# Scores of the fine levels of a chunked recurrence: four 32 by 32 products per block of 128 tokens in place of one 128 by 128 product

## The reference, cut to what matters

```python
def step(state, inp):
    q_, k_, v_, b_ = inp          # b_: cumulated log decay
    diff = jnp.where(causal[:, :, None], b_[:, :, :, None, :] - b_[:, :, None, :, :], -jnp.inf)
    a = jnp.einsum('bhtd,bhtsd,bhsd->bhts', q_, jnp.exp(diff), k_)
    o = a @ v_ + jnp.einsum('bhtd,bhde->bhte', q_ * jnp.exp(b_), state)
    ...
```

## Time and profile before

| | |
|---|---|
| three runs | 3310.64, 3315.96, 3316.32 us; median 3315.96 |
| profiled execution, its own time | 3312.84 us |
| its span, first to last instruction | 3311.0 us |
| mean granted TensorE clock | 0.996 |
| the stage of the change in the span | 2310.5 to 2364.4 us |

### The profile page before, as it was taken

The page is one execution under the profiler, slowest core; times in us unless marked ns, Lnnn a source line. Parts: engine busy times, 40 slices in busy tenths (PEclk is TensorE's granted clock), DMA queues, the critical chain, the costliest instruction groups (busy, mean ns, idle before and its releaser), DMA issues.

```text
span 3311.0 us, 48046 instructions
## 1 busy us (share of the span) xinstructions
PE 3235.8 (98%) x16228; PEld 2607.4 (79%) x16228; DVE 1928.3 (58%) x2441; ACT 1718.1 (52%) x2077; POOL 1338.8 (40%) x675
## 2 busy tenths in 40 slices
PE   8999999999999999999999999999989999999998
PEld 7888887678888788888778888778766788888784
DVE  4335684663355433461373333357667899999898
ACT  5552334545533555331445542523463788888884
POOL 3444442044444444444224444434301454445441
PEclk9999999999999999999999999999999999999999
DMA  3225331022244222443422223223103999999997
GB/s 128 95 97 165 125 105 58 8 91 99 95 146 152 83 95 95 141 157 108 131 86 95 95 96 96 100 82 106 59 9 125 367 377 384 388 388 388 371 368 303
DMA packets 128450, 534.38 MB, mean 161 GB/s; under 512 B 24433, under 2 KB 24689, under 8 KB 100465
## 3 DMA queue, kind: packets, MB, share of 16 engines
q1 hardware_dynamic: 107488, 499.63, 42.2%
q0 software_dynamic: 20736, 33.60, 2.7%
q10 hardware_dynamic: 144, 0.08, 0.0%
HBM read 531.64 MB, written 41.94 MB: 173 GB/s over the span
## 4 chain that ended last, share of the span: by engine, by line
PE 71%; issue 15%; POOL 5%; DVE 5%; DMA 3%; ACT 1%; POOLq 0%; DVEq 0%; SPq 0%; ACTq 0%
PE ps L881 20%; PE ps L883 20%; PE ps L882 20%; POOL w_lo L2099 5%; DMA big<-in_exp_gu 2%; PE ps L1448 2%; PE ps L1070 1%; PE ps L901 1%; PE ps L1080 1%; PE ps L1095 1%; DMA big<-slot_rows 1%; DVE hid L2870 1%; PE ps L1541 1%; PE ps L1200 1%; PE ps L1238 1%
## 5 line engine op out<-in xcount | busy, mean ns | idle before, releaser
L2099 POOL TENSOR_TENSOR w_lo<-stage_buf,w_hi 128x1024 fp32r<-128x1024 f32 (+1 forms) x396 | 968.6, 2446 | 1327.1 <-ACT w_hi L1629 1327.0
L1629 ACT ACTIVATE w_hi<-stage_buf 128x1024 fp32r<-128x1024 f32 (+1 forms) x396 | 414.1, 1046 | 1177.9 <-PE ps L883 1125.3
L881 PE MATMUL ps<-x_hi,w_hi 128*128 128x512 f32 x1984 | 773.4, 390 | 5.2 <-POOL w_lo L2099 3.3
L883 PE MATMUL ps<-x_hi,w_lo 128*128 128x512 f32 x1984 | 772.0, 389 | 0.0
L882 PE MATMUL ps<-x_lo,w_hi 128*128 128x512 f32 x1984 | 771.9, 389 | 0.0
L881 PE MATMUL ps<-hid,w_hi 128*128 128x512 f32 x1312 | 518.4, 395 | 3.0 <-issue 1.7
L883 PE MATMUL ps<-hid,w_lo 128*128 128x512 f32 x1312 | 511.6, 390 | 0.0
L882 PE MATMUL ps<-hid,w_hi 128*128 128x512 f32 x1312 | 510.8, 389 | 0.0
L881 PEld LDWEIGHTS ps<-x_hi,w_hi 128*128 128x128 f32 x1984 | 372.3, 188 | 86.7 <-POOL w_lo L2099 5.4
L883 PEld LDWEIGHTS ps<-x_hi,w_lo 128*128 128x128 f32 x1984 | 372.4, 188 | 77.9
L882 PEld LDWEIGHTS ps<-x_lo,w_hi 128*128 128x128 f32 x1984 | 372.4, 188 | 76.8
(11 more groups left out here) (404 smaller groups left out, 4783.6 us busy)
## 6 DMA issues: line engine op xcount, KB each, us to landing
stage_buf<-in_gu SPq DMA_DIRECT2D x176, 512.0 KB, 3.2
big<-in_exp_gu SPq DMA_DIRECT2D x72, 1024.0 KB, 12.0
h_buf<-in_exp_gu SPq DMA_DIRECT2D x72, 1024.0 KB, 12.0
s_buf<-in_exp_dn SPq DMA_DIRECT2D x72, 1024.0 KB, 11.1
stage_buf<-in_down SPq DMA_DIRECT2D x64, 512.0 KB, 3.6
stage_buf<-in_down SPq DMA_DIRECT2D x32, 384.0 KB, 3.2
sil_buf<-in_ada SPq DMA_DIRECT2D x24, 512.0 KB, 4.2
tmp_buf<-in_ada SPq DMA_DIRECT2D x24, 512.0 KB, 4.4
```

The source lines that it names most:

```text
L881: nc.tensor.matmul(o, a_hi, b_hi, start=start, stop=False)
L883: return nc.tensor.matmul(o, a_lo, b_hi, start=False, stop=stop)
L1629: nc.scalar.activation(w_hi[s][:, 0:n], stage[s][:, 0:n], ACT.Copy).then_inc(upper_done, 1)
L2099: nc.gpsimd.tensor_tensor(w_lo[s][:, 0:n], stage[s][:, 0:n], w_hi[s][:, 0:n].bitcast(F32), ALU.subtract).then_inc(parted, 1)
```

## The change

Where r is below 5, a block's 128 by 128 product becomes four products of 32 keys by 32 queries, on the diagonal of the block: 16 products per step in place of 4. The contraction stays 128 channels deep. Their outputs go to PSUM partitions 0, 32, 64 and 96, and cover the 32 by 32 squares on the diagonal; the rest of the bank keeps what was there, and the masks never select it. Nothing else is edited.

```diff
                     for t in range(TT):
                         if r < 5:
-                            c = slice(t * P, t * P + P)
-                            last = nc.tensor.matmul(o[:, c], hg_kw[:, hd, c], (hg_qw if r else q)[:, hd, c], start=True, stop=True)
+                            for a in range(0, P, 32):
+                                c = slice(t * P + a, t * P + a + 32)
+                                last = nc.tensor.matmul(o[a:a + 32, c], hg_kw[:, hd, c], (hg_qw if r else q)[:, hd, c],
+                                                        start=True, stop=True)
                         else:
                             half = 1 << (r - 1)
```

## The result

| | before | after |
|---|---|---|
| median of 22 executions each | 3314.18 us | 3319.53 us |
| lowest and highest | 3305.78, 3318.36 | 3306.79, 3330.51 |
| ratio after / before, 95% interval | | 1.0018, 1.0012 to 1.0024 |
| profiled execution, span | 3311.0 us | 3319.0 us |
| its mean granted clock | 0.996 | 0.991 |

The changed kernel is slower: the medians are 5.4 us apart, the ratio is estimated at 1.0018, and its interval doesn't reach 1. The forecast was 6.5 us faster, with a range up to 3315.5. Of the 22 executions of the changed kernel 21 have a mean clock of 0.992 or less and take 3315.8 us or more. The one that differs has 0.995 and takes 3306.79.

What follows compares the result with a forecast made beforehand. TensorE was taken to bound the kernel, and the stage except its last piece, which is VectorE's. Gains of 3.3 (steps 0 to 15), 0.9 (16 to 19) and 2.3 (20 to 25) sum to 6.5 us: 3309.5 us, range 3303.5 to 3315.5.

Steps and rivals of the forecast that it cites:

- What bounds the stage: Claimed TensorE bounds steps 0 to 15 and 20 to 25, and VectorE steps 26 to 31.
- what a step costs: Sixteen small products on four partition groups: 0.37 us a step, between 0.31 and 0.57.
- the 0.20 us of a change from small to whole products: L1344 after small products takes 1.04 us, not 0.84; without this the sum would be 2.2 us better.
- Steps 20 to 25: Six steps fall from some 0.92 us to 0.37, five pieces between get 0.20 each: gain 2.3 us.
- the piece behind them: Steps 26 to 31, where VectorE's queue ends the stretch: moves forward whole, unchanged in length.
- steps 0 to 15: First piece of the stage: 23.8 us in place of 27.1, gain 3.3 us, with waits for late weights.
- the rival of the clock: TensorE looks less busy, steps 8 to 16 above all; one or two low-clock stretches leave a gain of 3 to 5; chance 0.15.
- The slower outcome: Fixed start per record, or a clock low for most of the stage (slower from about 13 us on); chance 0.05.
- Steps 10 to 15 already ran so at 1.00: Argument against the clock rival: these steps, already with small products, ran at full clock in the kernel before.
- the weights' transfers: In steps 0 to 15 each load takes 3.19 us, 3.47 from last use to next, with waits of 0.3 us or so.
- The floor of about 25 ns from start to start: Skill page's limit on matmul starts: a step would take 0.8 us, the kernel about 3 us slower, 3319.

Runs made afterwards that it cites:

- early: Changed kernel with the small products only in steps 0 to 15, whole blocks in steps 16 to 31; 3323.51 us, ratio to before 1.0022.
- fill2: Changed kernel plus two products of zeros after each of steps 0 to 15; 3320.49 us, ratio to before 1.0004.
- fill_once: Changed kernel plus twelve products of zeros at step 4 alone; 3312.44 us, ratio to before 0.9993.
- twice: Changed kernel with every small product issued twice, to the same place; 3324.89 us, ratio to before 1.0030.
- fill_gaps: Changed kernel plus products of zeros, 12 at step 4 and 4 each at steps 6, 8, 10, 12, 14; 3312.09 us, ratio to before 0.9993.
- fill_all: Changed kernel plus products of zeros: 12 at step 4, 8 at step 8, 4 at steps 6, 10, 12, 14, 16 at step 19; 3310.26 us, ratio 0.9988.
- slow_weights: Kernel before, whole blocks, with two idle 512 KB transfers ahead of each of the last six weight loads; ratio to before 1.0066.
- wait_once: Kernel before, whole blocks, with one idle 512 KB transfer ahead of the third quarter's weights; 3316.55 us, ratio to before 1.0008.
- before_fill: Kernel before, whole blocks, plus nine products of zeros ahead of the far piece at step 19; 3313.86 us, ratio to before 0.9996.
- late: Changed kernel with the small products only in steps 16 to 31, whole blocks in steps 0 to 15; 3313.43 us, ratio to before 0.9996.

## Why the prediction was wrong

**What bounds the stage, and what a step costs: right.** 0.39 us a step where 0.37 was forecast, 1.03 for the products behind it where 1.04 was, the 0.20 us of a change from small to whole products among them. Steps 20 to 25 gained 2.3 us, as forecast, and VectorE ended the piece behind them: 9.03 us, 8.92 before. (Laid out again, the sum without the 0.20 us is 1.2 us better in steps 0 to 15, not 1.0; nothing rests on it.)

**The step that failed is the rival of the clock, in its price and its chance.** The sum charges nothing for the clock, and the rival charges one or two short stretches: "A stretch like that one, on the path, costs up to half of itself, 1.7 us. One or two more": it took the length of a low stretch from the one in the earlier trace rows, which ended after some 3.4 us. In the loop it doesn't end: 30.7 us in the changed kernel and in early, 34 in fill2's profile, 37.5 and 44.4 with whole blocks. In all seven profiles where it fell in the loop (fill_once and twice are the other two) it rose again 3.3 to 5.7 us after the start of step 16, among other pieces than the loop's. Steps 0 to 15 were forecast 3.3 us shorter and came out 8.9 longer, 12.2 us apart. The instructions that ran at the lower level there cost some 11.5 us more than the same ones at 1.00 (ten times L1346 at 1.90 in place of 1.03 are 8.7 of them), and the longer wait at step 4 is most of the rest. The slower outcome that I gave, "a clock that stays low for most of the stage" (for over 13 us), is what happened; it had a chance of less than 0.05.

**The evidence against it was read too generously.** "Steps 10 to 15 already ran so at 1.00" was true of steps without a long wait in them. What I forecast myself, light steps and waits for weights in one place, is what before doesn't have there. The runs fit the two adding up: 2 of 13 are low with one longer wait alone, 21 of 22 with both, 5 of 12 where step 4's wait is filled, none of 12 where most are. They don't prove it: a filler takes away a wait and gives TensorE more work at once, and the small products without any wait were never run.

**A term of the sum was mis-sized: the weights' transfers.** The 3.19 us of one load was used for all. The load that step 4 waited for took 4.34, 4.73 in fill_once. At the kept clock steps 0 to 15 took 27.3 us in fill_gaps and 27.8 in fill_all, not 23.8. Without any wait or filler the sixteen steps come to 23.0 us, and the forecast put 0.9 us of waiting on top. In fill_gaps late loads are 2.9 us on top (steps 4 and 8), in fill_all 4.1 (steps 4, 8, 10 and 14); the products of zeros where no load was late are the other 1.4 and 0.7. So the forecast's gain of 3.3 us is not seen in any profile. Executions that weren't traced do better: the five of fill2 at 0.995 or more have a median of 3306.5 us, where before's 25 with such a clock, run beside them, have 3314.6; the six of fill_once have 3308.5 beside 3312.5. With the clock kept, a gain of the forecast's size happens, but not each time: fill_all's nine have 3310.1 beside 3313.3.

**What makes a load late.** The traces show a coincidence that is close to an answer. The profiles but slow_weights have 144 loads of 512 KB into the staging buffers issued from 2295 to 2350 us; leave out the one in wait_once that had the idle transfer ahead of it. 26 of the 143 took 4.1 us or more, and beside every one a 16 KB packet of the instruction queue began between 0.2 us before its issue and 3.0 after. The 17 where it began 0.7 to 2.5 us after the issue all took 4.2 to 5.3. The 99 with no such packet took 3.0 to 4.0. And it isn't chance at step 4: its load took 4.2 to 4.9 us in all seven profiles that have the 32 by 32 products there once (changed, early and the five filled ones), each with such a packet beside it, and 3.2 to 3.3 in before, before_fill and late, without one. So the added records seem to have made the load late that the clock fell behind. The trace of the kernel before had the warning: its load issued at 2307.37, with a packet beside it, took 4.86 us. No run moved these packets alone, so the cause isn't shown.

**The Trainium skill's rules.** TensorEngine Tiling (Array Packing), Key Properties, on the drain between tiling modes, agrees with the 0.20 us, now in the changed kernel too. The floor of about 25 ns from start to start (TensorE: Matmul & The Clock Gate) doesn't hold for the new step: 32 records in 0.39 us are 12 ns each. The same page, Part 1, has a section on oscillation: a kernel whose TensorE falls back to the low clock at every wait for transfers, at a cost of half the time spent low. The price agrees (L1346 at 1.90 us for 1.03). What differs is that here one fall lasted as long as the loop, 30.7 us.

**What stays open.** Why some executions of one program fall and others don't: 5 and 6 of 12 in fill2, and the wait of 2.19 us that a fall meets in fill_gaps and not in late. Whether the instruction packets cause the late loads and the "issue" waits of twice. And the 2.7 us behind the stage: low stretches are seen there, but that part, which no kernel here edits, differs by more than that among the profiles. That the fall of the clock is the cause of the loss is shown by the instructions' own times at the two levels, by the kept clock in late, fill_gaps and fill_all, none of which is slower than before, and by fill2's two kinds of executions. What makes it fall is in part argued.

## What to carry to other kernels

Work taken from TensorE in a loop that also waits for transfers is not free even where nothing depends on it: look at what the loop then does in its lightest few microseconds, and price a low clock by the length of the loop, not by the length of the low stretches that the old trace happens to show. Before a change that makes TensorE's steps shorter, ask which load becomes late, and take the slowest load of that size in the old trace, not the one in the chain. Four times the instructions are also more instruction packets beside those loads. Where the clock decides, compare the clocks of many executions; one profile shows only one of two kinds. And cheap products of zeros in the waits can win back what was lost: 3312.1 and 3310.3 us in fill_gaps and fill_all, 3319.5 without them.

## What the runs showed of the hardware that was not expected

The low clock holds itself. With whole blocks, TensorE busy without a gap for 17.2 us (wait_once from 2320.97 to 2338.20: 2.02 and 1.81 us, one after the other), the clock stayed at 0.50, where the same sequence of instructions had run at 1.00 for 8 us before the wait, and for 17.9 us in the kernel before. Sixteen 32 by 32 products on four partition groups (0.39 us) cost hardly more than eight on two (0.37); thirty-two took 0.69 to 0.72. Twice as many small products brought "issue" waits of 0.8 us into the stage, where neither the kernel before nor the changed one has any (both have some of 0.8 us elsewhere, at L881). A 512 KB load with a 16 KB instruction packet beginning 0.7 to 2.5 us behind its issue took 4.2 to 5.3 us, one with none beside it 3.0 to 4.0.
